# One GpSimd instruction per weight unit in place of four: the low half of a split weight stream, in a chain of two transformer blocks

## The reference, cut to what matters

```python
z = rms_norm(x, norm_mix_w) @ w_in + b_in
x = x + mixed @ w_out
x = x + jnp.square(jax.nn.relu(h2 @ w_ff1)) @ w_ff2      # first block, twice
h = h + merged @ w_out
return h + (jax.nn.silu(a_part) * b_part) @ w_ffn_out    # second block, once
```

## The kernel before, in words

| line | reads | who waits for it |
|---|---|---|
| L1908 to L1915, angles of the rotary embedding (16 in a row, each waits for the one before) | SBUF | L1869 behind them in the queue, then TensorE's L323 |
| L774, L777, L781, rotary embedding | two SBUF tensors; PSUM and one; two | the next one; TensorE's L823 after the last |
| L867, scores plus mask | PSUM and one SBUF tensor | ACT's exponential L900 |
| L880, probabilities times the reciprocal sum, two per step | one SBUF tensor | TensorE's transposes L847 |
| L966, conv of four taps | three SBUF operands | ACT |
| L1092, L1096 scans over the gates, L1098 | two SBUF tensors | L1100, then TensorE's L1076 |
| L1203, L1207, L1215, decay matrix of the mLSTM | one; two; PSUM and one | ACT's L1293; TensorE's next scores L1161 |
| L1333, gate | PSUM and one SBUF tensor | ACT |
| L1400, `mixed_lo` | two SBUF tensors | TensorE's L299 |
| L2177, then L2787 behind it in the queue | one SBUF tensor; PSUM | TensorE's L1044 |

## Time and profile before

### The profile page before, as it was taken

How to read it: one execution, slowest core, us unless ns; L and a number is a source line. 1 busy time by engine, 2 the same in 40 slices (tenths; PEclk the granted TensorE clock), 3 DMA queues, 4 the chain that set the end, 5 groups by cost and what they waited for, 6 DMA issues and landing times.

```text
span 2598.0 us, 30131 instructions
## 1 busy us (share of the span) xinstructions
PE 2488.6 (96%) x11731; PEld 2007.7 (77%) x11731; DVE 991.5 (38%) x1578; ACT 872.5 (34%) x1090; POOL 1115.7 (43%) x808
## 2 busy tenths in 40 slices
PE   6999999999999998999999999889898799999998
PEld 5867788888888867788888887788675488888887
DVE  4446544311202446553311203548484424322201
ACT  4255233421323255233422323442324323322213
POOL 3433245454544433244554543532242245455543
PEclk8999999999999999999999999988999899999999
DMA  4212222323323222123222223220221122232221
GB/s 134 82 50 65 65 81 97 97 98 97 97 97 96 71 61 70 50 84 100 92 97 97 97 97 98 66 65 25 71 73 58 53 81 98 97 97 97 97 97 65
DMA packets 174011, 215.16 MB, mean 83 GB/s; under 512 B 7644, under 2 KB 155028, under 8 KB 173908
## 3 DMA queue, kind: packets, MB, share of 16 engines
q1 hardware_dynamic: 171412, 209.86, 25.1%
q10 hardware_dynamic: 2496, 3.83, 0.4%
HBM read 211.19 MB, written 2.10 MB: 82 GB/s over the span
## 4 chain that ended last, share of the span: by engine, by line
issue 47%; POOL 28%; PE 23%; DVE 1%; POOLq 0%; ACT 0%; DVEq 0%
POOL w_lo L276 28%; PE ps L706 6%; PE ps L308 3%; PE ps L306 3%; PE ps L307 3%; PE ps L1695 2%; PE ps L1697 2%; PE ps L1693 2%; PE ps L847 0%; PE ps L823 0%; PE ps L834 0%; DVE att_negscores L867 0%; POOLq L278 0%; PE ps L2255 0%; DVE s_window L2282 0%
## 5 line engine op out<-in xcount | busy, mean ns | idle before, releaser
L276 POOL TENSOR_TENSOR w_lo<-w_raw,w_hi 128x512 fp32r<-128x512 f32 x804 | 1115.5, 1419 | 1455.7 <-ACT w_hi L267 1455.7
L267 ACT ACTIVATE w_hi<-w_raw 128x2048 fp32r<-128x2048 f32 x201 | 384.8, 1915 | 1079.4 <-PE ps L308 393.2
L706 PE MATMUL ps<-h_hi,w_hi 128*128 128x512 f32 (+1 forms) x936 | 401.3, 429 | 11.1 <-POOL w_lo L276 6.2
L706 PE MATMUL ps<-h_hi,w_lo 128*128 128x512 f32 (+1 forms) x936 | 372.9, 398 | 0.0
L706 PE MATMUL ps<-h_lo,w_hi 128*128 128x512 f32 (+1 forms) x936 | 372.6, 398 | 0.0
L306 PE MATMUL ps<-h_hi,w_hi 128*128 128x512 f32 x816 | 319.0, 391 | 0.0
L308 PE MATMUL ps<-h_hi,w_lo 128*128 128x512 f32 x816 | 317.5, 389 | 0.0
L307 PE MATMUL ps<-h_lo,w_hi 128*128 128x512 f32 x816 | 317.4, 389 | 0.0
L706 PEld LDWEIGHTS ps<-h_hi,w_hi 128*128 128x128 f32 (+1 forms) x936 | 178.7, 191 | 77.8 <-issue 31.5
L706 PEld LDWEIGHTS ps<-h_lo,w_hi 128*128 128x128 f32 (+1 forms) x936 | 178.9, 191 | 44.5 <-issue 8.9
L706 PEld LDWEIGHTS ps<-h_hi,w_lo 128*128 128x128 f32 (+1 forms) x936 | 178.0, 190 | 42.6
(11 more groups left out here) (399 smaller groups left out, 3677.9 us busy)
## 6 DMA issues: line engine op xcount, KB each, us to landing
w_raw<-in_w_in SPq DMA_DIRECT2D x72, 1024.0 KB, 5.2
w_raw<-in_w_ff SPq DMA_DIRECT2D x64, 1024.0 KB, 5.2
w_raw<-in_w_ffn_in SPq DMA_DIRECT2D x22, 1024.0 KB, 5.0
w_raw<-in_w_out SPq DMA_DIRECT2D x12, 1024.0 KB, 5.0
w_raw<-in_w_ffn_out SPq DMA_DIRECT2D x11, 1024.0 KB, 4.9
w_raw<-in_w_proj_att SPq DMA_DIRECT2D x4, 1024.0 KB, 5.0
w_raw<-in_w_proj_mlstm SPq DMA_DIRECT2D x4, 1024.0 KB, 5.0
w_raw<-in_w_up_ssd SPq DMA_DIRECT2D x4, 1024.0 KB, 5.6
```

The costliest lines, as they stand in the source:

```text
L267: act.activation(k.whi[:, slot * SLOT:(slot + 1) * SLOT], k.wraw[:, slot * SLOT:(slot + 1) * SLOT], ACT.Copy).then_inc(k.hi_done, 1)
L276: ins = pool.tensor_tensor(k.wlo[:, a:a + T], k.wraw[:, a:a + T], k.whi[:, a:a + T], ALU.subtract)
L706: mm = pe.matmul(out, lhs, rhs, start=i == 0 and n == 0, stop=stop and n == 2)
```

## The change

Per unit, the four subtractions of 128x512 elements become one of 128x2048. The elements, the wait before them and the semaphore count after them stay. 804 instructions become 201.

```diff
     def one(slot, value):
+        a = slot * SLOT
         pool.wait_ge(k.hi_done, value)
-        for a in range(slot * SLOT, (slot + 1) * SLOT, T):
-            ins = pool.tensor_tensor(k.wlo[:, a:a + T], k.wraw[:, a:a + T], k.whi[:, a:a + T], ALU.subtract)
-        ins.then_inc(k.split, 1)
+        pool.tensor_tensor(k.wlo[:, a:a + SLOT], k.wraw[:, a:a + SLOT], k.whi[:, a:a + SLOT],
+                           ALU.subtract).then_inc(k.split, 1)
```

## The result

| | before | after |
|---|---|---|
| median (lowest to highest) | 2604.31 us (2599.86 to 2606.66) | 2667.47 us (2664.76 to 2670.45) |
| profiled execution, span | 2599.86 us, 2598.0 us | 2666.07 us, 2664.2 us |
| TensorE busy, rest of the span | 2488.6 us, 109.4 us | 2510.7 us, 153.5 us |
| mean granted clock | 0.981 | 0.971 |

The changed kernel is slower: the ratio is 1.024, with a 95% interval of 1.0223 to 1.0257. Between the two profiled executions the difference is 66.2 us. The third line of the table splits it: 44.1 us are idle time of TensorE, 22.1 us are the same 11731 matmuls taking longer, at a lower clock. Of the runs behind the experiments' table, one of the ten executions of e1 took 2832.05 us at a granted clock of 0.838 (the other nine 2597.25 to 2605.47) and is in no ratio.

A forecast was written before the change was run, and what follows sets the result against it. TensorE was 96% busy, almost never waiting for GpSimd, but GpSimd and VectorE hold each other up. Stalls 45.4 + 9.9, gain -0.9 and clock +9 make 63, taken as +60 on 2599.86: 2660 us, range 2640 to 2680.

The forecast's parts named there:

- Rival A: GpSimd passes the port on inside the 2048 columns, so VectorE waits as now: 2598 us, chance 0.09.
- start-up: Units 0 and 1 delay the angle operations and L1869, for which TensorE's L323 waits: +3.8 us, once.
- rotary embedding: L774 of the last tile is caught at 123.7, so TensorE's L823 starts later: +3.0 us, twice.
- attention, three units: L880 caught in three units per layer, delaying TensorE by 3.3, 2.5 and 2.7 us: +8.5, twice.
- gates: mLSTM gates: the caught scan ends 2.1 us later, L1098 is no longer caught (-0.5): +1.6 us, twice.
- mLSTM scores: L1207 caught in the unit at 275.12, L1215 after it, delaying TensorE's L1161 at 277.73: +2.8 us, twice.
- nine small: Nine similar places with less time to lose (mLSTM, softplus, first feed-forward units), each priced at 1.1: +9.9 us.
- The clock: Eleven new stalls of 2.5 us and more each bring a lower-clock stretch, 0.8 us each: +9, bounds 0 and 19.
- B: Faster: VectorE has slack everywhere, so all 9.6 us of TensorE's waits for GpSimd could go: 2590 us, chance 0.06.
- C: Half: terms resting on no present wait (27 us) are absorbed by slack, the clock's 9 stay away: 2624 us, chance 0.2.
- D: More: H at 5.04 (+8), full clock cost per long stall (+10), side work stopped: 2690 us, chance 0.1.
- H: Length of a unit as one 2048-column subtraction on GpSimd: taken as 4.6 us, 5.04 if nothing is saved.

The follow-up runs named there:

- e1: Changed kernel's single 2048-column subtraction only in the 82 feed-forward units, four of 512 elsewhere: 2601.51 us, ratio 0.9996 to the kernel before.
- e3: Every unit as two subtractions of 1024 columns, otherwise the changed kernel: 2639.50 us, ratio 1.0137 to the kernel before.
- e4: Every unit as eight subtractions of 256 columns, otherwise the changed kernel: 2593.10 us, ratio 0.9964 to the kernel before.
- e9: Every unit as sixteen subtractions of 128 columns, otherwise the changed kernel: 2592.51 us, ratio 0.9965 to the kernel before.
- e8: Every unit as two subtractions, first 512 then 1536 columns, otherwise the changed kernel: 2643.40 us, ratio 1.0161 to the kernel before.
- e12: Changed kernel, but the ten units under rotary embedding and attention are four subtractions of 512 columns: 2623.35 us, ratio 1.0079 to the kernel before.
- e2: Changed kernel's single subtraction only in ten units under rotary embedding and attention, four of 512 elsewhere: 2643.78 us, ratio 1.0159 to the kernel before.
- e7: Every unit as two subtractions, first 1536 then 512 columns, otherwise the changed kernel: 2641.20 us, ratio 1.0154 to the kernel before.

## Why the prediction came out as it did

Forecast 2660 us, measured 2667.47. The mechanism, who is held up by what and where TensorE pays for it, was right at all places but one; the split between stalls and clock was not, and two opposite errors brought the sum close.

- *Length of a unit.* 4.6 us was forecast, 4.608 is the median, 4.501 the shortest. The fixed cost, taken from VectorE as 0.157, measured 0.14 on GpSimd: (5.04 - 4.61) / 3.
- *VectorE kept out for the whole instruction.* Right: maxima of 4.64 (L880) and 4.69 us (L1207), L1333 unmoved, and in e3, e4 and e9 L880's maximum goes down with the size of the piece. Rival A, a hold given up inside an instruction, is out. The Trainium skill (SBUF — State Buffer, section "SBUF: two separate sides") says that the shared pair is an exclusive lock for the whole instruction; the trace agrees, 4.82 us for two operations issued 0.2 us after a subtraction of 4.50 us began.
- *One wait for a row of operations.* "Where several follow one another only the first waits, instead of each one once" was right for one long piece (the two L880 above). Pricing two pieces in e3 and e8 I forgot its other half, that with more pieces each one waits.
- *The places.* TensorE's start of the same instruction, after minus before, and how far it moves at each place:

| place | forecast | measured |
|---|---|---|
| start-up | 3.8 | 4.2, of which 1.9 are left at 80 us |
| rotary embedding | 3.0, twice | 3.1, 3.1 |
| attention, three units | 8.5, twice | 9.2, 9.2 |
| gates | 1.6, twice | 0.3, 1.1 |
| mLSTM scores | 2.8, twice | 0, 0 |
| output projection | 1.1, three times | 1.1, 1.1, 1.1 |
| SSD to selection | 3.5 | 3.2 |
| attention, second block | 3.0 | 2.9, of which 0.6 come back |
| nine small | 9.9 | 8.9 |

The last line of the table is mLSTM 0.9 and 1.1 in each layer, softplus 0.9 once, the first feed-forward units 1.1 three times, and 0.8 in the second block's attention. The stalls came to 44.1 us of idle time, forecast 54.4 (45.4 + 9.9 - 0.9). The measured column adds up to 48.5, since some of these moves are longer busy time (of the 1.1 us at the first feed-forward unit 0.5 are idle). At the gates the scan L1092 grew by the 2 us forecast (1.45 and 1.44 us before, 3.48 and 3.50 after), but L1096 and L1098 behind it, no longer caught, gave back 1.1 instead of 0.5.

- *The step that failed among the stalls: mLSTM scores.* L1207 is caught as described, and for 4.56 us. But the L1161 at 277.73 doesn't wait for what stands behind it. The next one does, at 282.00 before: by the code a score waits for the L1215 of two steps earlier, which follows the caught L1207 in VectorE's queue and had ended at 277.26. VectorE, then TensorE, after the change:

```profile
298.28 4.56 DVE L1207 TENSOR_TENSOR mlstm_decay<-mlstm_decay,constants 128x128 f32<-128x128 f32 x1
302.76 0.68 DVE L1215 SCALAR_TENSOR_TENSOR mlstm_weighted<-ps,mlstm_decay 128x512 f32<-128x512 f32 x1
```
```profile
303.49 0.70 PE L1161 MATMUL ps<-conv_out 128*128 128x256 f32 x2
```

L1215 ends at 303.44 and L1161 starts at 303.49, but TensorE has no idle time in front of it: side work (L706) fills the gap, and the 4.7 us of slack were just enough. Before the change L1207 had been caught twice there, 1.25 and 1.24 us. I had tied a late operation to the next score in time instead of to the one that waits for it: 5.6 us too much.

- *Rotary embedding, right by another way.* The prediction has L774 of the last tile caught. What was caught is L781 of the tile before. The unit began at 125.05, and L781 at 125.11, 0.06 us late; before the change, L781 was in at 123.10 and the unit at 123.16. The price is the same, because L774 then waits for nothing. It also shows how much of such a term hangs on phase: in e12, with short units here, the wait of L823 is 1.50 us instead of 0.33 (before).

```profile
125.11 5.06 DVE L781 TENSOR_TENSOR qk<-rope_cos,rope_sin 128x512 f32<-128x512 f32 x1
```

- *Start-up.* The price was right at L323. That only 1.9 of the 4.2 us are left at 80 us is no slack: before, the granted clock from 57.6 to 61.0 us was 0.50, in the changed kernel's profiled execution it was 1.00. e2, with the short units of before at the start, gained 2.4 us in the same stretch, and e12, with long ones there, kept 4.1. So the give-back is an accident of the executions compared.
- *The clock, the term that was mis-sized.* +9 was forecast (bounds 0 and 19), 22.1 us of busy time is what came, in one execution each. From the mean clock, TensorE was at the lower level for 2598.0 x 0.019 / 0.5 = 99 us before and 2664.2 x 0.029 / 0.5 = 155 us after, so 56 us more. I had put at most one stretch of 3.4 us behind each of eleven stalls, 37 us in all, and half of its cost, "since part lies beside VectorE's chains". Both were too low. In the stretch of attention shown above the stalls of 3.42, 4.43, 3.11 and 2.71 us end at 132.2, 152.5, 179.0 and 202.5 us. The granted clock fell within about a microsecond of each of these ends. Here are the windows (stretch, busy us of each engine, granted clock) of the lower level:

```profile
131.90:135.30 3.40, 3.08 (x10) 2.37 (x11) 0.78 (x5) 1.73 (x4) 0.00 (x0) 0.51 0.00 0
152.40:155.80 3.40, 3.32 (x10) 2.63 (x11) 0.35 (x2) 0.49 (x1) 0.00 (x0) 0.50 0.72 214
179.80:186.50 6.70, 6.30 (x18) 4.80 (x19) 2.17 (x8) 1.63 (x6) 0.00 (x0) 0.50 0.50 156
203.60:207.00 3.40, 3.40 (x10) 1.14 (x9) 2.13 (x7) 1.52 (x4) 0.00 (x0) 0.50 0.91 302
```

That is 17 us at the lower level for four places, one of them of double length, and TensorE is busy for 16.1 of them, so nearly the full half is lost: an estimate of 8 us, where the forecast has 3.2 (4 x 0.8). Of the 56 us more, e2, with long units only at rotary embedding and attention, has 44 (2640.2 x 0.027 / 0.5 = 143 us in all). What makes the clock fall stays open. The sum of the stalls doesn't decide it: e7 has more added idle time (32.9 us) than e8 (27.1) and e3 (25.2), and loses less busy time over before, 8.3 us against 19.2 and 21.0. The executions' spread (2.7 us from e8's median, 6.5 from e3's) takes off a part of this distance, not all. In attention of the first layer the clock was 0.94 (e3, stalls of 3.4, 2.3 and 1.9 us) and 0.95 (e7: 3.4, 3.3, 2.0). It stayed at 1.00 in e12, with stalls of 1.5 and 1.2 us:

```profile
120.00:232.00 112.00, 105.60 (x602) 74.46 (x601) 58.90 (x152) 55.31 (x120) 31.08 (x18) 1.00 0.16 48
```

- *The rivals.* B, faster, has no support: the four waits for GpSimd fell from 9.6 to 8.6 us, about the 0.9 forecast, and nothing else was gained. Of C's list only the mLSTM terms, 5.6 of 27 us, were absorbed; the rest (182.68, 422.75, 1989.61, most of the small ones) came at full price. D named the clock's higher cost, and that part of it came true; its H of 5.04 didn't.

The two misses have opposite signs, 10 us too much in stalls and 13 too little in the clock. That the forecast is nearer than its parts is luck.

## What to carry to other kernels

Where VectorE and GpSimd both work from SBUF, the length of one GpSimd instruction is how long a VectorE operation can be kept out, so its size is a question of who stands behind VectorE and not of GpSimd's own fixed costs (here 0.14 us each): join instructions in stretches where nobody waits for VectorE, and cut them where TensorE does. If cut, cut fine: a pair of operations against two pieces waits for both. There is an end to it: sixteen pieces gained no more than eight here. And price a stall on TensorE with the clock that it may take along: here 44 us of waiting brought 22 us of slower matmuls.

## What the runs showed of the hardware

- GpSimd's two-input subtraction of 128 columns took a median of 460 ns, of 256 columns 737, of 1024 2402, of 2048 4608: some 2.2 ns for a column. A unit alone took 6.73 us in sixteen pieces, 5.04 in four and 4.61 in one.
- In the other direction, GpSimd can be put behind for very long. In every one of the kernels one of its instructions took 11 to 19 us under VectorE's unbroken row of L966 (15051 ns before, 18557 after, 16247, 19168 and 11239 with 1024, 256 and 128 columns).
- The port changes hands in two ways. A pair of L880, one behind the other in the queue, was parted by a piece of GpSimd's (e8: 1.26 and 3.63 us, against pieces of 1.27 and 3.59), so one operation got in per seam. In the row of L966, from 16 (e9) to 27 (e4) VectorE operations started while one piece was waiting. What makes the difference was not tried.
- ScalarE's operations on the same SBUF data didn't wait for GpSimd: at most 713 ns with short and 714 with long subtractions, and 38.7 us of TensorE's waits for them with either.
- In the changed kernel four stalls of TensorE, of 2.71 to 4.43 us, were each followed by about 3.4 or 6.7 us at a granted clock of 0.50; in e12, with stalls of 1.5 and 1.2 us in the same stage, it stayed at 1.00.
